# Differential attention: scores of two units in a row, packed into three PSUM banks per unit

## The chip, the cores and the metric

The program runs on one core of one Trainium2 chip. The metric is the device time of one execution in microseconds (us), the median of several. The core has five engines that this text speaks of by the profile's names: PE (TensorE; its weight loads are listed apart as PEld), DVE (VectorE), ACT (ScalarE), POOL (GpSimd) and SP (which issues DMAs). Each works through its own instructions in order, and they are tied to one another by semaphores.

## The reference, cut to what matters

The program computes two whole networks, one after the other: two layers of a first block (retention, sparse attention, gating, feed-forward), and then two layers of a second (gated delta rule, feed-forward, differential attention, feed-forward). The change lies in differential attention alone. There, each of 8 heads has two score maps with 64 numbers per key; the second map's softmax is subtracted from the first's with a learned factor, and the difference weighs the values.

```python
DA_HEADS = 8; DA_DIM = 64; DA_QBLOCK = 128        # 512 queries, 512 + 256 keys
k_all = jnp.concatenate([kl, kc], axis=3)
v_all = jnp.concatenate([vl, vc], axis=2)

def attend(q, k, v):
    s = jnp.einsum('cbhqd,cbhkd->cbhqk', q, k).astype(f32)   # c: the two maps
    p = jax.nn.softmax(s, axis=-1)
    a = p[0] - lam_val * p[1]
    return jnp.einsum('bhqk,bhkv->bhqv', a, v.astype(f32))
```

All of it is float32, and what comes out is 512 x 1024 numbers.

## The kernel before, in words

The program is a row of stages. Each stage has one function per engine (`da_pe`, `da_act`, `da_dve`, `da_pool` for the stage of this text), written out by hand in the order in which that engine shall work; a stage ends with a barrier (`stage_end`) at which the stage's semaphores are cleared. No planner decides anything. Queries, keys and values lie in SBUF when the stage begins, and the stage issues no DMA.

The stage has 32 units (`AUNITS`, L3596): 8 heads times 4 blocks of 128 queries. For each unit u the steps are these.

- **Scores** (`scores`, L3607 to 3619, PE): four matmuls, two maps times the keys in pieces of 512 and 256. A map has 64 rows to contract, so map 0 uses the upper 64 rows of the array and map 1 the lower 64. Each float32 matmul appears in the trace as two passes. A map of a unit has a buffer of two PSUM banks, and there are three such buffers (`da_scores`, L3655): one and a half units.
- **Lowest** (`lowest`, L3696, DVE): the queries were scaled by a negative number, so the smallest of 768 scores is wanted, for each map.
- **Exp** (L3680, ACT): the exponential of a map, with its sum over the keys read out behind it. The sum signals `p_ready`, which frees the score buffer. The results lie in SBUF, in one of three buffers (`k.ap`).
- **Factor and combination**: DVE forms the reciprocals of the two sums (L3716) and the factor of the second map (L3717). Then DVE adds factor times map 1 to map 0 for keys 0 to 383 (L3724), and POOL does so for keys 384 to 767 in two instructions (L3738 a product, L3739 a sum).
- **Turn** (`turn`, L3629, PE): the combination is transposed in two halves of three 128 x 128 blocks. Both halves go into the same PSUM bank, bank 6, so each turn waits until ACT has copied the one before it out (`turned_half`, L3670, signalling `pt_ready`).
- **Weigh** (`weigh`, L3638, PE): six matmuls with the values, into bank 7. DVE scales the result (L3703) and sums its squares (L3710).

PE's order in one round u is scores(u), first turn of u-2, weigh(u-3), second turn of u-2. ACT's order is copy of the first turn of u-2, exp of map 0 of u, exp of map 1 of u, copy of the second turn of u-2. DVE's order is the scaling of u-4, lowest of map 0, squares of u-4, reciprocals and factor of u-1, lowest of map 1, combination of u-1.

Of the kernel before, what the change touches and what calls it, by code (L numbers as in the profile page):

```python
# [25 lines left out]
P = 128  # L26
# [114 lines left out]
class Semaphores:  # L141


    def __init__(self, nc):
        sem = nc.alloc_semaphore
# [22 lines left out]
        self.o_taken = sem("o_taken")  # L168
        self.vsq_ready = sem("vsq_ready")
        self.p_ready = sem("p_ready")  # L170
        self.factor_ready = sem("factor_ready")
        self.s_ps = sem("s_ps")
        self.ov_taken = sem("ov_taken")
# [378 lines left out]
def spin_pe(k, pe, moving, bank, n):  # L552

    for _ in range(n):
        signal_later(k, pe.matmul(k.ps[:, bank, :], k.ident, moving, start=True, stop=True))
# [1559 lines left out]
SEGS = ((0, 512, 0), (512, 256, 516))  # L2115
# [1481 lines left out]
KEYS = NT2 * P  # L3597
# [5 lines left out]
def da_pe(k, e, slot, _):  # L3603
    pe, S = e.eng, k.S
    n = len(AUNITS)

    def scores(u):  # L3607
        h, i = AUNITS[u]
        if u >= 2:
            pe.wait_ge(S.p_ready, 2 * u - 1)  # L3610
        elif u == 1:
            pe.wait_ge(S.p_ready, 1)
        for at, m, _ in SEGS:
            for c in range(2):
                rows = slice(64 * c, 64 * c + 64)
                last = pe.matmul(da_scores(k, u, c)[:, at:at + m], k.aq[rows, h, i * P:(i + 1) * P],  # L3616
                                 k.ak[rows, h, at:at + m], start=True, stop=True)
                if at:
                    last.then_inc(S.s_ps, 1)

    def turn(v, part):
        if part == 0:
            pe.wait_ge(S.combined, v + 1)
            pe.wait_ge(S.combined_pool, v + 1)
        if v or part:
            pe.wait_ge(S.pt_ready, 2 * v + part)
        for j in range(3):
            at = HALF_KEYS * part + j * P
            last = pe.transpose(k.ps[:, 6, j * P:(j + 1) * P], k.ap[v % 3][:, 0, at:at + P], k.ident)  # L3629
        last.then_inc(S.pt_ps, 1)  # L3630

    def weigh(v):
        h, i = AUNITS[v]
        pe.wait_ge(S.pt_ready, 2 * v + 2)
        if v:
            pe.wait_ge(S.ov_taken, v)
        for j in range(NT2):
            last = pe.matmul(k.ps[:, 7, 0:P], k.apt[v % 2][:, j * P:(j + 1) * P], k.av[:, j, h * P:(h + 1) * P],  # L3638
                             start=j == 0, stop=j == NT2 - 1)
        last.then_inc(S.ov_ps, 1)  # L3640

    spin_pe(k, pe, k.c2[:, 0:512], 7, 1)
    for u in range(n + 3):
        if u < n:
            scores(u)
        if 2 <= u < n + 2:
            turn(u - 2, 0)
        if u >= 3:
            weigh(u - 3)
        if 2 <= u < n + 2:  # L3650
            turn(u - 2, 1)
    spin_pe(k, pe, k.c2[:, 0:512], 0, 3)


def da_scores(k, u, c):  # L3655

    b = 2 * ((2 * u + c) % 3)
    return k.ps[:, b:b + 2, :].rearrange("p a b -> p (a b)")[:, 0:KEYS]


def da_act(k, e, _):
    act, S = e.eng, k.S
    n = len(AUNITS)

    def turned_half(v, part):
        act.wait_ge(S.pt_ps, 2 * v + part + 1)
        if v >= 2 and part == 0:
            act.wait_ge(S.ov_ps, v - 1)
        at = HALF_KEYS * part
        act.activation(k.apt[v % 2][:, at:at + HALF_KEYS], k.ps[:, 6, 0:HALF_KEYS], ACT.Copy).then_inc(S.pt_ready, 1)  # L3670

    for u in range(n + 2):
        for c in range(2):
            if u >= 2 and c == 0:
                turned_half(u - 2, 0)
            if u < n:
                act.wait_ge(S.o_ps, 2 * u + c + 1)
                if u >= 3 and c == 0:
                    act.wait_ge(S.pt_ps, 2 * (u - 2))
                act.activation(k.ap[u % 3][:, c, :], da_scores(k, u, c), ACT.Exp, bias=k.amin[:, 2 * u + c:2 * u + c + 1],  # L3680
                               scale=-1.0, accum_out=k.asum[:, 2 * u + c:2 * u + c + 1]).then_inc(S.p_ready, 1)
            if u >= 2 and c == 1:
                turned_half(u - 2, 1)
    act.activation(k.small[:, 254:255], k.eps, ACT.Sqrt)
    act.wait_ge(S.head_ms_ready, 1)
    act.activation(k.small[:, 64:64 + 8 * NT1], k.small[:, 64:64 + 8 * NT1], ACT.Sqrt).then_inc(S.head_std_ready, 1)


def da_dve(k, e, _):
    dve, S = e.eng, k.S  # L3690
    n = len(AUNITS)

    def lowest(u, c):
        at = 2 * u + c
        dve.wait_ge(S.s_ps, at + 1)
        dve.tensor_reduce(k.amin[:, at:at + 1], da_scores(k, u, c), AX.X, ALU.min).then_inc(S.o_ps, 1)  # L3696

    for u in range(n + 4):
        if u >= 4:
            v = u - 4  # L3700
            h, i = AUNITS[v]
            dve.wait_ge(S.ov_ps, v + 1)
            dve.tensor_scalar(k.amix[:, i, h * P:(h + 1) * P], k.ps[:, 7, 0:P], k.arec[:, 2 * v:2 * v + 1],  # L3703
                              None, ALU.mult).then_inc(S.ov_taken, 1)
        if u < n:
            lowest(u, 0)
        if u >= 4:
            unit = k.amix[:, i, h * P:(h + 1) * P]
            dve.wait_ge(S.ov_taken, v + 1)
            dve.tensor_tensor_reduce(out=k.asq, in0=unit, in1=unit, scale=1.0, scalar=0.0, op0=ALU.mult, op1=ALU.add,  # L3710
                                     accum_out=k.small[:, 8 * i + h:8 * i + h + 1]).then_inc(S.head_sq_summed, 1)
        if 1 <= u <= n:
            v = u - 1
            rec, fac = k.arec[:, 2 * v:2 * v + 2], k.afac[:, v:v + 1]
            dve.wait_ge(S.p_ready, 2 * v + 2)
            e.link(dve.reciprocal(rec, k.asum[:, 2 * v:2 * v + 2]))  # L3716
            dve.scalar_tensor_tensor(fac, rec[:, 1:2], k.asum[:, 2 * v:2 * v + 1], k.lamt[:, 133:134],  # L3717
                                     ALU.mult, ALU.mult).then_inc(S.factor_ready, 1)
        if u < n:
            lowest(u, 1)  # L3720
        if 1 <= u <= n:
            p = k.ap[v % 3][:, :, 0:HALF_KEYS]
            dve.wait_ge(S.factor_ready, v + 1)
            dve.scalar_tensor_tensor(p[:, 0, :], p[:, 1, :], fac, p[:, 0, :], ALU.mult, ALU.add).then_inc(S.combined, 1)  # L3724
    part = 1.0 - LAMBDA_INIT
    dve.wait_ge(S.head_sq_summed, n)
    dve.tensor_scalar(k.small[:, 64:64 + 8 * NT1], k.small[:, 0:8 * NT1], 1.0 / (P * part ** 2), EPS / part ** 2, ALU.mult,
                      ALU.add).then_inc(S.head_ms_ready, 1)
    dve.wait_ge(S.head_std_ready, 1)
    dve.reciprocal(k.small[:, 0:8 * NT1], k.small[:, 64:64 + 8 * NT1])  # L3730
# [280 lines left out]
```

## Time and profile before

| what | value |
|---|---|
| median of 3 runs | 3542.41 us (3542.16 to 3545.89) |
| the profiled execution | 3539.66 us |
| its span in the trace | 3537.9 us |
| the stage of the change, from its first scores to the barrier's end | 2961.3 to 3094.0, 132.7 us |
| busy in that stretch: PE, DVE, ACT, POOL | 120.5, 102.1, 91.5, 66.9 us |
| granted TensorE clock in that stretch, share of full speed | 1.00 |

The profile is of one execution. Its own time stands beside its span because 1.8 us of it lie before the first and behind the last instruction that the trace has. Times within the trace count from the span's start. PE's busy time includes the drain of each matmul, which lies beside the next matmul; so how long PE needs for a step is read from the start of one group of matmuls to the start of the next.

### The profile page before, as it was taken

To read this page: it belongs to the slowest core of one execution; us is meant where nothing else is said; L and a number is where in the kernel's file an instruction comes from. 1 tells how busy PE (TensorE), PEld (TensorE's weight loads), DVE (VectorE), ACT (ScalarE), POOL (GpSimd) and SP (SyncE) were. 2 spreads that over 40 slices of the span, in tenths; PEclk is the share of its full clock that TensorE was granted. 3 is DMA by queue.
4 is the path that set the end of the run, shared out by engine and by line. 5 is a ranking of instruction groups with operands and counts; after the bars stand their busy time and mean duration, and the time that the engine had idled before them with its cause. 6 is when DMAs were issued, how large, how long until landed. Compare 5 with 4: busy or idle time off the path is not lost.

```text
span 3537.9 us, 57598 instructions
## 1 busy us (share of the span) xinstructions
PE 3409.8 (96%) x24652; PEld 2813.1 (80%) x24652; DVE 2083.2 (59%) x2894; ACT 823.1 (23%) x1551; POOL 341.6 (10%) x311
## 2 busy tenths in 40 slices
PE   8999999999999999999998999999999999999998
PEld 6777888877778888878888977888888686678886
DVE  4665777746657776756665666422245754764347
ACT  1243001222530012542252221000021204610021
POOL 0000000000100000025205500300000002502000
PEclk9999999999999999999999999999999999999999
DMA  4311544423025443210010041111111331022222
GB/s 177 109 37 50 206 186 165 147 95 108 25 77 196 185 160 124 105 38 3 32 60 3 4 161 60 60 60 61 71 60 72 112 111 36 1 84 95 97 100 90
DMA packets 51454, 320.48 MB, mean 91 GB/s; under 512 B 7132, under 2 KB 7644, under 8 KB 16648
## 3 DMA queue, kind: packets, MB, share of 16 engines
q1 hardware_dynamic: 30492, 220.50, 17.0%
q10 hardware_dynamic: 20716, 96.36, 7.6%
q8 instruction: 195, 3.19, 0.4%
q14 instruction: 51, 0.42, 0.0%
HBM read 299.94 MB, written 9.56 MB: 87 GB/s over the span
## 4 chain that ended last, share of the span: by engine, by line
PE 79%; DVE 7%; PEld 6%; DMA 3%; issue 2%; ACT 2%; PEldq 1%; POOL 0%; POOLq 0%; ACTq 0%; another core or an unknown queue 0%; DVEq 0%; SPq 0%
PE psum L561 20%; PE psum L562 20%; PE psum L563 20%; PE psum L2633 4%; PE psum L2640 3%; DMA pieces_in<-pieces 2%; PEld psum L561 2%; PEld psum L563 2%; PEld psum L562 2%; PE psum L1404 1%; PE psum L1388 1%; PE psum L758 1%; PE psum L1377 1%; PE psum L3616 1%; DVE xt_values L3696 1%
## 5 line engine op out<-in xcount | busy, mean ns | idle before, releaser
L561 PE MATMUL psum<-xt_operands,pieces_hi 128*128 128x512 f32 (+1 forms) x2544 | 938.6, 369 | 19.4 <-DVE xt_operands L818 8.4
L562 PE MATMUL psum<-xt_operands,pieces_hi 128*128 128x512 f32 (+1 forms) x2544 | 927.9, 365 | 0.0
L563 PE MATMUL psum<-xt_operands,pieces_lo 128*128 128x512 f32 (+1 forms) x2544 | 927.1, 364 | 0.0
L561 PEld LDWEIGHTS psum<-xt_operands,pieces_hi 128*128 128x128 f32 x2544 | 480.9, 189 | 106.7 <-issue 15.2
L561 PE MATMUL psum<-pieces_hi,xt_operands 128*128 128x512 f32 x1338 | 532.2, 398 | 15.5 <-DVE pieces_lo L608 10.6
L563 PEld LDWEIGHTS psum<-xt_operands,pieces_lo 128*128 128x128 f32 x2544 | 480.8, 189 | 77.2
L562 PEld LDWEIGHTS psum<-xt_operands,pieces_hi 128*128 128x128 f32 x2544 | 481.3, 189 | 73.4
L562 PE MATMUL psum<-pieces_lo,xt_operands 128*128 128x512 f32 x1338 | 524.5, 392 | 0.0
L563 PE MATMUL psum<-pieces_hi,xt_operands 128*128 128x512 f32 x1338 | 524.2, 392 | 0.0
L618 DVE TENSOR_TENSOR pieces_lo<-pieces_in,pieces_hi 128x2048 fp32r<-128x2048 f32 x190 | 443.5, 2334 | 5.3
L575 DVE CAST pieces_hi<-pieces_in 128x2048 fp32r<-128x2048 f32 x190 | 237.5, 1250 | 301.6 <-PE psum L561 154.6
L561 PEld LDWEIGHTS psum<-pieces_hi,xt_operands 128*128 128x128 f32 x1338 | 253.4, 189 | 74.7 <-DVE pieces_lo L608 12.6
L562 PEld LDWEIGHTS psum<-pieces_lo,xt_operands 128*128 128x128 f32 x1338 | 253.6, 190 | 54.3 <-issue 2.4
L563 PEld LDWEIGHTS psum<-pieces_hi,xt_operands 128*128 128x128 f32 x1338 | 253.5, 189 | 53.6
L1667 ACT ACTIVATE arena<-psum 128x512 f32<-128x512 f32 x66 | 39.5, 598 | 673.8 <-PE psum L563 673.8
L1703 DVE TENSOR_TENSOR arena<-psum,arena 128x512 f32<-128x512 f32 x66 | 45.6, 691 | 247.1 <-ACT arena L1667 247.1
L3460 DVE TENSOR_TENSOR arena<-psum,arena 128x768 f32<-128x768 f32 x22 | 21.1, 957 | 256.1 <-ACT arena L3427 256.1
L2442 DVE SCALAR_TENSOR_TENSOR x_mem<-x_mem,arena 128x772 f32<-128x772 f32 x96 | 98.2, 1023 | 66.8 <-ACT x_mem L2341 64.2
L2633 PE MATMUL psum<-arena 128*128 128x128 f32 x976 | 129.2, 284 | 0.0
L2633 PEld LDWEIGHTS psum<-arena 128*128 128x128 f32 x976 | 115.7, 193 | 6.1 <-DVE x_mem L2910 3.1
L1770 DVE SCALAR_TENSOR_TENSOR arena<-x_mem,xt_values,arena 128x2048 f32<-128x2048 f32 x44 | 101.9, 2345 | 3.3 <-DMA x_mem<-ada 3.3
L1684 ACT ACTIVATE xt_operands<-arena 128x512 fp32r<-128x512 f32 x102 | 59.8, 625 | 184.4 <-PE psum L561 145.0
(391 smaller groups left out, 4048.0 us busy)
## 6 DMA issues: line engine op xcount, KB each, us to landing
pieces_in<-pieces SPq DMA_DIRECT2D x210, 1024.0 KB, 4.8
x_mem<-ada ACTq DMA_DIRECT2D x28, 1024.0 KB, 4.9
arena<-ada ACTq DMA_DIRECT2D x20, 1024.0 KB, 4.8
arena<-mods ACTq DMA_DIRECT2D x8, 512.0 KB, 15.7
arena<-arena ACTq DMA_DIRECT2D x32, 128.0 KB, 4.9
xt_values<-arena ACTq DMA_DIRECT2D x8, 384.0 KB, 9.1
x_park<-x_mem ACTq DMA_DIRECT2D x1, 3072.0 KB, 14.4
o_park<-arena ACTq DMA_DIRECT2D x2, 1536.0 KB, 5.1
```

What stands on the lines that cost most here:

```text
L561: signal_later(k, pe.matmul(out, sh, mh, start=start, stop=False))
L562: signal_later(k, pe.matmul(out, sh, ml, start=False, stop=False))
L563: return pe.matmul(out, sl, mh, start=False, stop=stop)
L575: e.link(dve.tensor_copy(k.hi[n % 2], k.ring[i]))
L618: e.eng.tensor_tensor(k.ring_lo[i], k.ring[i], k.hi[n % 2].bitcast(F32), ALU.subtract).then_inc(k.S.lo_ready, 1)
L1667: act.activation(silu[:, f % 2, 0:nt * P], k.ps[:, 2 * (f % 2), 0:nt * P], ACT.Silu).then_inc(S.silu_ready, 1)
L1684: act.activation(hs[j % len(hs)][0], hid[:, j % FT, :], ACT.Copy).then_inc(S.hs_hi_ready, 1)
L1703: dve.tensor_tensor(hid[:, f, 0:nt * P], k.ps[:, 2 * (f % 2) + 1, 0:nt * P], silu[:, f % 2, 0:nt * P], ALU.mult).then_inc(S.hid_taken, 1)
L1770: eng.scalar_tensor_tensor(total, weights, c, total, ALU.mult, ALU.add).then_inc(added, 1)
L2442: ins = dve.scalar_tensor_tensor(conv, raw[:, j:j + 772], taps[:, n, j:j + 1], conv, ALU.mult, ALU.add)
L2633: last = pe.matmul(out, lhs(s, d, h), rhs(s, d, h), start=True, stop=True)
L2640: last = pe.matmul(out[r, h, :], lhs(h, r), rhs(h, r), start=True, stop=True)
```

## The change

Three things are altered, all in this stage.

The score buffers: a unit now has three PSUM banks, banks 0 to 2 or 3 to 5, in turn. The 768 scores of map 0 are followed at once by the 768 of map 1, so the middle bank is shared: its first half belongs to map 0, its second to map 1. Two units fit, and both maps of a unit are handed on together: the first lowest and the first exp of a unit wait for both maps (`s_ps` and `o_ps` at 2u+2), and the scores of u wait for both exps of u-2.

The order of a unit's matmuls: map 0's 512 keys, map 1's 256 (which fall into the middle bank), map 1's 512, map 0's 256 (also the middle bank). Before the last, PE waits on a new semaphore until map 1's 256 have been written.

The order of the steps: PE does the scores of units p and p+1, and then first turn, weigh, second turn of p-2 and of p-1. DVE does both lowest of a unit next to each other, ahead of the squares. ACT's order is as it was.

```diff
     def scores(u):
+
         h, i = AUNITS[u]
         if u >= 2:
-            pe.wait_ge(S.p_ready, 2 * u - 1)
-        elif u == 1:
-            pe.wait_ge(S.p_ready, 1)
-        for at, m, _ in SEGS:
-            for c in range(2):
-                rows = slice(64 * c, 64 * c + 64)
-                last = pe.matmul(da_scores(k, u, c)[:, at:at + m], k.aq[rows, h, i * P:(i + 1) * P],
-                                 k.ak[rows, h, at:at + m], start=True, stop=True)
-                if at:
-                    last.then_inc(S.s_ps, 1)
+            pe.wait_ge(S.p_ready, 2 * u - 2)
+        for c, at, m in ((0, 0, 512), (1, 0, 256), (1, 256, 512), (0, 512, 256)):
+            rows = slice(64 * c, 64 * c + 64)
+            if (c, at) == (0, 512):
+                pe.wait_ge(S.middle_bank_written, u + 1)
+            last = pe.matmul(da_scores(k, u, c)[:, at:at + m], k.aq[rows, h, i * P:(i + 1) * P],
+                             k.ak[rows, h, at:at + m], start=True, stop=True)
+            if at:
+                last.then_inc(S.s_ps, 1)
+            elif c == 1:
+                last.then_inc(S.middle_bank_written, 1)
...
-    for u in range(n + 3):
-        if u < n:
-            scores(u)
-        if 2 <= u < n + 2:
-            turn(u - 2, 0)
-        if u >= 3:
-            weigh(u - 3)
-        if 2 <= u < n + 2:
-            turn(u - 2, 1)
+    for pair in range(0, n + 2, 2):
+        if pair < n:
+            scores(pair)
+            scores(pair + 1)
+        for v in (pair - 2, pair - 1):
+            if v >= 0:
+                turn(v, 0)
+                if v >= 1:
+                    weigh(v - 1)
+                turn(v, 1)
+    weigh(n - 1)
...
-    b = 2 * ((2 * u + c) % 3)
-    return k.ps[:, b:b + 2, :].rearrange("p a b -> p (a b)")[:, 0:KEYS]
+    b = 3 * (u % 2)
+    return k.ps[:, b:b + 3, :].rearrange("p a b -> p (a b)")[:, KEYS * c:KEYS * c + KEYS]
...
-                act.wait_ge(S.o_ps, 2 * u + c + 1)
+                act.wait_ge(S.o_ps, 2 * u + 2)
...
-        dve.wait_ge(S.s_ps, at + 1)
+        dve.wait_ge(S.s_ps, 2 * u + 2)
...
         if u < n:
             lowest(u, 0)
+            lowest(u, 1)
...
-        if u < n:
-            lowest(u, 1)
```

On PE, one round in the middle of the stage stood in this order before (L3616 scores, L3629 a turn, L3638 a weigh; every wait is in brackets, a row with x2 or x5 holds the rest of its group):

```order
L3616 MATMUL psum<-arena 128x512 [waits p_ready]
L3616 MATMUL psum<-arena 128x512
L3616 MATMUL psum<-arena 128x256 x2
L3629 MATMUL psum<-arena,xt_values 128x128 [waits pt_ready,combined_pool,combined]
L3629 MATMUL psum<-arena,xt_values 128x128 x2
L3638 MATMUL psum<-arena,xt_values 128x128 [waits ov_taken,pt_ready]
L3638 MATMUL psum<-arena,xt_values 128x128 x5
L3629 MATMUL psum<-arena,xt_values 128x128 [waits pt_ready]
L3629 MATMUL psum<-arena,xt_values 128x128 x2
```

Now the same place reads as follows, from the second unit's scores of a pair on (L3617 scores, L3632 a turn, L3641 a weigh):

```order
L3617 MATMUL psum<-arena 128x512 [waits p_ready]
L3617 MATMUL psum<-arena 128x256
L3617 MATMUL psum<-arena 128x512
L3617 MATMUL psum<-arena 128x256 [waits middle_bank_written]
L3632 MATMUL psum<-arena,xt_values 128x128 [waits pt_ready,combined_pool,combined]
L3632 MATMUL psum<-arena,xt_values 128x128 x2
L3641 MATMUL psum<-arena,xt_values 128x128 [waits ov_taken,pt_ready]
L3641 MATMUL psum<-arena,xt_values 128x128 x5
L3632 MATMUL psum<-arena,xt_values 128x128 [waits pt_ready]
L3632 MATMUL psum<-arena,xt_values 128x128 x2
L3632 MATMUL psum<-arena,xt_values 128x128 [waits pt_ready,combined_pool,combined]
L3632 MATMUL psum<-arena,xt_values 128x128 x2
```

The second turn of one unit is now followed at once by the first turn of the next, with no scores between them, and the wait for `pt_ready` of that first turn is for ACT's copy of the turn just ahead of it.

On DVE, one round stood in this order before (L3703 scaling, L3696 lowest, L3710 squares, L3716 and L3717 reciprocals and factor, L3724 combination):

```order
L3703 TENSOR_SCALAR xt_values<-psum,xt_values 128x128 [waits ov_ps]
L3696 TENSOR_REDUCE xt_values<-psum 128x1 [waits s_ps]
L3710 ISA xt_values,arena<-xt_values 128x128 [waits ov_taken]
L3710 ISA arena 128x1
L3716 RECIPROCAL xt_values<-xt_values 128x2 [waits p_ready]
L3717 SCALAR_TENSOR_TENSOR xt_values<-xt_values,arena 128x1 [waits dve_chain]
L3696 TENSOR_REDUCE xt_values<-psum 128x1 [waits s_ps]
L3724 SCALAR_TENSOR_TENSOR xt_values<-xt_values 128x384 [waits factor_ready]
```

Now it reads (L3708 scaling, L3701 lowest, L3716 squares, L3722 and L3723 reciprocals and factor, L3728 combination):

```order
L3708 TENSOR_SCALAR xt_values<-psum,xt_values 128x128 [waits ov_ps]
L3701 TENSOR_REDUCE xt_values<-psum 128x1 [waits s_ps] x2
L3716 ISA xt_values,arena<-xt_values 128x128 [waits ov_taken]
L3716 ISA arena 128x1
L3722 RECIPROCAL xt_values<-xt_values 128x2 [waits p_ready]
L3723 SCALAR_TENSOR_TENSOR xt_values<-xt_values,arena 128x1 [waits dve_chain]
L3728 SCALAR_TENSOR_TENSOR xt_values<-xt_values 128x384 [waits factor_ready]
```

The factor of the unit before, for which POOL waits, now stands behind both lowest of the new unit, and the combination stands right behind the factor.

## Rows read from the trace of the kernel before

**Rows 1.** The profile's page, its first line.

```profile
span 3537.9 us, 57598 instructions
```

**Rows 2.** Windows: stretch, length, busy per engine, granted clock, DMA share, GB/s.

```profile
2961.30:3094.00 132.70, 120.50 (x839) 86.33 (x838) 102.08 (x258) 91.49 (x195) 66.86 (x64) 1.00 0.01 5
2962.00:2970.00 8.00, 3.86 (x24) 1.67 (x20) 4.46 (x7) 3.86 (x8) 1.97 (x2) 1.00 0.05 22
```

**Rows 3.** Timeline about a round without a gap: start, duration, engine, line, what.

```profile
3014.14 1.56 PE L3616 MATMUL psum<-arena 64*128 64x512 f32 x8
...
3014.68 0.19 PEld L3616 LDWEIGHTS psum<-arena 64*128 64x128 f32 x2 [0.24 <-issue]
...
3015.11 0.19 PEld L3616 LDWEIGHTS psum<-arena 64*128 64x128 f32 x2 [0.23 <-issue]
...
3015.67 0.52 PE L3629 MATMUL psum<-arena,xt_values 128*128 128x128 f32 x3
3015.74 0.96 DVE L3696 TENSOR_REDUCE xt_values<-psum 128x1 f32<-128x768 f32 x1 [0.83 <-PE psum L3616]
...
3016.03 1.50 PE L3638 MATMUL psum<-arena,xt_values 128*128 128x128 f32 x12
3016.23 0.49 ACT L3670 ACTIVATE xt_values<-psum 128x384 f32<-128x384 f32 x1 [0.70 <-PE psum L3629]
3016.61 0.28 DVE L3710 CUSTOM_DVE_ANT_0 xt_values<-xt_values 128x128 f32<-128x128 f32 x1
...
3016.82 0.16 DVE L3716 RECIPROCAL xt_values<-xt_values 128x2 f32<-128x2 f32 x1
3017.01 0.22 DVE L3717 SCALAR_TENSOR_TENSOR xt_values<-xt_values,arena 128x1 f32<-128x1 f32 x1
...
3017.37 0.49 PE L3629 MATMUL psum<-arena,xt_values 128*128 128x128 f32 x3
...
3017.79 0.70 PE L3616 MATMUL psum<-arena 64*128 64x512 f32 x2
```

**Rows 4.** Timeline about the round ahead of it, which has a gap on PE.

```profile
3010.16 1.56 PE L3616 MATMUL psum<-arena 64*128 64x512 f32 x8
...
3010.51 0.90 ACT L3680 ACTIVATE xt_values<-psum,xt_values 128x768 f32<-128x768 f32 x1 [0.41 <-DVE xt_values L3696]
3010.59 1.26 POOL L3739 TENSOR_TENSOR xt_values<-xt_values 128x384 f32<-128x384 f32 x1
...
3011.40 0.48 ACT L3670 ACTIVATE xt_values<-psum 128x384 f32<-128x384 f32 x1
...
3012.03 0.52 PE L3629 MATMUL psum<-arena,xt_values 128*128 128x128 f32 x3 [0.30 <-ACT xt_values L3670]
...
3012.58 0.49 ACT L3670 ACTIVATE xt_values<-psum 128x384 f32<-128x384 f32 x1 [0.70 <-PE psum L3629]
...
3012.97 0.90 ACT L3680 ACTIVATE xt_values<-psum,xt_values 128x768 f32<-128x768 f32 x1
```

**Rows 5.** Timeline at the stage's start: the first scores, the first two lowest.

```profile
2961.37 1.56 PE L3616 MATMUL psum<-arena 64*128 64x512 f32 x8
...
2962.96 1.82 DVE L3696 TENSOR_REDUCE xt_values<-psum 128x1 f32<-128x768 f32 x2 [3.20 <-PE psum L3616]
```

**Rows 6.** Groups of instructions by line within the stage: busy us, mean ns.

```profile
L3724 DVE SCALAR_TENSOR_TENSOR xt_values<-xt_values 128x384 f32<-128x384 f32 x32 | 20.1, 629 | 0.0
```

**Rows 7.** Timeline at the stage's end: the last unit, and the last weigh.

```profile
3084.37 0.22 DVE L3717 SCALAR_TENSOR_TENSOR xt_values<-xt_values,arena 128x1 f32<-128x1 f32 x1
...
3084.63 1.28 DVE L3724 SCALAR_TENSOR_TENSOR xt_values<-xt_values 128x384 f32<-128x384 f32 x1
...
3084.67 0.83 POOL L3738 TENSOR_TENSOR xt_values<-xt_values 128x384 f32<-128x384 f32 x1 [0.57 <-DVE xt_values L3717]
...
3085.57 1.19 POOL L3739 TENSOR_TENSOR xt_values<-xt_values 128x384 f32<-128x384 f32 x1
...
3089.90 1.27 PE L3638 MATMUL psum<-arena,xt_values 128*128 128x128 f32 x9 [0.58 <-ACT xt_values L3670]
```

More of the change, by code:

```diff
@@ L170, in __init__ @@
         self.p_ready = sem("p_ready")
+        self.middle_bank_written = sem("middle_bank_written")
         self.factor_ready = sem("factor_ready")
```

## The prediction

> **What bounds the kernel now.** I read the page first: one execution spans 3537.9 us [rows 1]. The change touches one stage, so I cut it out with the view of windows: 132.7 us, in which PE is busy 120.5, DVE 102.1, ACT 91.5 and POOL 66.9 us [rows 2]. The reader is to see that PE is close to full there, but that no engine is far behind, so that the order of the steps can decide. The chain of waits was next: in this stretch it goes round through PE's scores, DVE's lowest, ACT's exp and copy, and PE's turn, weigh, turn, once in two rounds. The timeline then gives the steps. I count PE by the starts of its groups. In one round scores to turn takes 1.53 us (3014.14 to 3015.67), turn to weigh 0.36, weigh to turn 1.34, turn to the next scores 0.42: 3.65 us without a gap [rows 3]. The round ahead of it takes 3.98 us (3010.16 to 3014.14), since its first turn comes 0.30 us late, behind ACT's copy [rows 4]. Two rounds are 7.63 us. So before, PE does 7.30 us of work in 7.63, and what there is to win is that 0.33 and whatever the regrouping saves on PE.
>
> **What it removes.** The wait of scores for an exp of the unit just before goes, since two whole units now have buffers; in the middle of the stage it cost nothing that the rows show. Scores that follow scores lose the cost of going from whole-array work to half-array work and back. The passes of one piece of 512 keys start 0.43 us apart (3014.68 to 3015.11) [rows 3], a piece of 256 should take 0.21, and two passes of each make 1.28 us for a unit, the two maps side by side. So the first scores of a pair should take 1.28 instead of 1.53, and one turn-to-scores step of 0.42 becomes a turn-to-turn step of about 0.36. Gain per pair: 0.25 + 0.06 = 0.31 us.
>
> **The new matmul order inside a unit.** Each map still has 768 keys in two passes, so 1.28 us if both halves of the array stay busy. Map 0's last 256 keys wait for the semaphore of map 1's first 256, which should have been streamed after 0.43 us, while map 0's first 512 need 0.85. This wait is covered by about 0.4 us. The trace shows no wait of PE on its own matmul here, so bounds: below, 1.28 us, because the columns are the same; above, no overlap of the halves at all, 2.56 us. I take 1.28, nearest to the row in which eight passes fit into 1.56 us [rows 3].
>
> **What it adds.** In a pair, the second turn of unit p-2 is followed at once by the first turn of p-1, which uses the same bank 6. It cannot start until ACT has copied the second turn out, and scores no longer lie between. ACT's order is unchanged, and this is what makes the wait long: the copy of the second turn stands behind both exps of unit p, these stand behind the copy of the first turn of p-2, and that turn now stands behind the scores of two units. Counted from the start of the pair's first scores:
>
> - ACT's path: scores 1.28 + 1.53 = 2.81 to the first turn; turn to copy 0.56 (3015.67 to 3016.23) [rows 3]; copy to exp 0.39 (3012.58 to 3012.97), exp to the copy behind it 0.89 (3010.51 to 3011.40), which I also take for exp to exp, and copy to turn 0.63 (3011.40 to 3012.03) [rows 4]. Sum: 2.81 + 0.56 + 0.39 + 0.89 + 0.89 + 0.63 = 6.17 us.
> - DVE's and POOL's path. The same turn also waits until POOL has combined unit p-1. POOL waits for the factor, and DVE now makes that behind both lowest of unit p. Scores to lowest 1.60 (3014.14 to 3015.74) [rows 3]; two lowest take 1.82 with 0.95 for the last, so each holds DVE 0.87 [rows 5], together 1.74; squares to reciprocals 0.21, reciprocals to factor 0.19 [rows 3]; factor to POOL's product 0.30, product to sum 0.90 [rows 7]; the sum 1.26, and from its end to the turn at most 0.18 (3011.85 to 3012.03) [rows 4]. There ACT's copy ended 0.03 us later than POOL, so I take 0.15. Sum: 1.60 + 1.74 + 0.21 + 0.19 + 0.30 + 0.90 + 1.26 + 0.15 = 6.35 us.
>
> The later one decides: the second unit's first turn at 6.35 us. PE would be ready for it at 2.81 + 0.36 + 1.34 + 0.36 = 4.87, so it stands idle for 1.48 us. Behind it 0.36 + 1.34 + 0.42 = 2.12, and the next pair begins at 8.47 us. Against 7.63 that is 0.84 us more for each pair. Queued on PE behind that waiting turn are a weigh, a turn and the next pair's scores, and for these wait DVE's next lowest, and so everything.
>
> **Side costs.** DVE's combination now starts right behind the factor, beside POOL's product. At the stage's end, where the order happens to be that, it took 1.28 us (3084.63); the mean of all 32 is 629 ns, so the other 31 took (32 x 0.629 - 1.28) / 31 = 0.61 us [rows 6, 7]. I expect about 1.28 us for all 32. It costs nothing by itself: the combination is not on POOL's path, and it is followed by the next unit's lowest, whose exps ACT reaches only at about 7.3 us. DVE then has per pair four lowest of 0.87 and twice about 2.3 us of the rest, some 8.1 of 8.47, so it is nearly full; if it grew by 0.4 us it would be the bound. PE's clock: in the stage's first 8 us, with PE busy for 3.86 of them, the granted clock stayed at 1.00, the level of 2.4 GHz [rows 2]; an idle 1.48 us in 8.47 should leave it there.
>
> **The sum.** Fill, from the same steps: exps of unit 0 at 3.5 and 4.3, scores 2 at 5.4 (an exp of 0.90 and a hand-over of 0.14), exps of unit 1 at 5.2 and 6.1, scores 3 at 7.1, first turn 8.7, copy 9.2, exps of unit 2 at 9.6 and 10.5, copy 11.4, turn of unit 1 at 12.0, scores 4 at 14.2 us. Then 13 pairs to scores 30: 13 x 8.47 = 110.1. Then the end, counted from scores 30: factor of unit 30 at 7.8 (behind a combination of 1.28 from 4.0 on, a scaling and two lowest), POOL's sum done at 10.3, its turns at 10.4 and 12.1, copy and turn of unit 31 at 12.7 and 13.3, its second turn 15.0, copy 15.6, last weigh 16.2. Together 14.2 + 110.1 + 16.2 = 140.5 us from first scores to last weigh. Before it is 3089.90 - 2961.37 = 128.5 us [rows 5, 7]. So +12.0 us. The profiled execution took 3539.66 us and should become 3551.7; it lies 2.8 us under the median of the runs shown, 3542.41, against which I forecast 3554.4 us.
>
> **Rivals.**
>
> *The scores lose their side-by-side.* For it: in-order issue, and a wait in the middle of the unit that was not there. Against it: the cover of 0.4 us. If map 0's last 256 keys came wholly by themselves, 0.43 us for each scores, ACT's path would be 6.17 + 0.86 = 7.03 and the pair 9.15: 13 x 1.52 + 3 = 23 us, 3565 us. With no overlap at all: 6.17 + 2.56 = 8.73, the pair 10.85, about +49 us, 3591 us. Chance 12%.
>
> *DVE and POOL hold each other longer than the combination shows.* If the squares too were held by the 0.67 us that the combination loses (1.28 against 0.61), POOL's path would be 7.02 and the pair 9.14: 13 x 0.67 = 8.7 more, 3563 us. Against it: the squares stand where POOL should be idle. Chance 8%.
>
> *Only bank 6 counts.* If the copy of the second turn found ACT free, the second unit's turn would come at 2.81 + 0.36 + 1.34 + 0.56 + 0.63 = 5.70, the pair at 7.82: 13 x 0.19 and about 1 us for fill and end, +3.5 us, 3546 us. It needs both paths 0.5 to 0.7 us shorter than their rows. Chance 7%.
>
> *Faster: PE was the bound, and the regrouping pays.* If the second unit's turn did not wait at all, a pair would be 4.87 + 2.12 = 6.99 us, 0.64 less than now: 16 x 0.64 = 10 us, 3532 us. It decides as soon as the idle time ahead of that turn is under 0.64 us instead of 1.48. For it: PE is the fullest engine, and half of the changes between half-array and whole-array work go. Against it: even a free ACT leaves 5.70 - 4.87 = 0.83 us of idle time, for the bank alone. Chance 4%. The Trainium skill (TensorEngine Tiling (Array Packing), Key Properties) says that a change of tiling mode drains TensorE. By that rule alone the change must win, since it halves the changes of mode. The rows agree on a cost, but a small one: scores to turn is 1.53 where the passes make 1.28, of which some is the first weight load [rows 3].
>
> **How the numbers follow.** The forecast has 69%. Its own range: the pair between 8.29 (ACT's path alone) and 8.65 (scores of 1.40), thus +9.5 to +14.5 us, and with 2 us for the scatter of the runs 3550 to 3559. The range for 8 in 10 goes up to the first of the rivals and down a little, 3548 to 3565 us. About 0.2% (7 us) is what a measurement of this kernel can tell from no change. Slower by more than that: forecast less a small part, and the first two rivals, 88%. Within it: the third rival and a little, 8%. Faster: 4%.
>
> **What would show it.** Right, step by step: in the middle of the stage scores to scores 1.28 us inside a pair and a pair of 8.47; the second unit's first turn idle for about 1.5 us, released by ACT's copy or POOL; the copy of second turns directly behind the second exp of an even unit; combinations of about 1.28 us; the granted clock at 1.00. The stage's first scores to last weigh should be 140.5 us and every other stage as before. Wrong: a pair under 7.9 us, or idle time ahead of the second unit's turn of less than 0.8 us; scores to scores over 1.6 us would point to the first rival.

## The result, and the profile after

The changed kernel takes 3565.57 us (median of 5 runs, 3561.94 to 3573.47), the kernel before 3545.89 us beside it (5 runs, 3542.16 to 3552.71). The ratio is 1.0057, with a 95% interval of 1.0038 to 1.0076: slower, by about 20 us. The forecast was 3554.4 us with a range up to 3565; counted as a rise it was 12.0 us, and 19.7 were measured.

The profiled execution took 3565.57 us, 25.9 more than that of before. Two stretches hold the difference. In the changed stage, first scores to last weigh is 3115.63 - 2967.24 = 148.4 us where before had 128.5, so +19.9. Another 6.2 us lie in an early stage that the change does not touch (all the rest together is 0.2 us shorter). The view of windows shows that stage, before first and then after (columns as in [rows 2]):

```profile
878.50:984.60 106.10, 100.37 (x962) 78.88 (x962) 66.98 (x264) 51.40 (x126) 12.35 (x28) 1.00 0.09 31
```

```profile
878.30:990.60 112.30, 106.62 (x962) 84.40 (x962) 67.04 (x264) 51.39 (x126) 12.40 (x28) 0.94 0.08 29
```

The same 962 matmuls and the same work on DVE, ACT and POOL, but a granted clock of 0.94 instead of 1.00. That is scatter of one execution: three of the changed kernels below (wait kept with its own bank, old order, spin matmuls) had 1.00 in this stage. And the ratio of the medians, worth 20 us, agrees with the changed stage alone. So all that follows is read inside the stage.

The timeline of the changed kernel shows a pair of units in the middle of the stage, the answer to [rows 3, 4] (start, duration, engine, line, what, and in brackets the idle time before and what ended it; L3617 scores, L3632 a turn, L3675 its copy, L3685 exp, L3743 POOL's sum):

```profile
3019.19 0.73 PEld L3617 LDWEIGHTS psum<-arena 64*128 64x128 f32 x6 [0.17 <-ACT xt_values L3685]
3019.19 3.52 PE L3617 MATMUL psum<-arena 64*128 64x512 f32 x16
...
3020.39 0.83 PEld L3617 LDWEIGHTS psum<-arena 64*128 64x128 f32 x8 [0.46 <-PE psum L3617]
...
3022.02 0.29 PEld L3617 LDWEIGHTS psum<-arena 64*128 64x128 f32 x2 [0.80 <-PE psum L3617]
...
3022.64 0.55 PE L3632 MATMUL psum<-arena,xt_values 128*128 128x128 f32 x3
...
3023.23 0.49 ACT L3675 ACTIVATE xt_values<-psum 128x384 f32<-128x384 f32 x1 [2.96 <-PE psum L3632]
...
3023.61 0.90 ACT L3685 ACTIVATE xt_values<-psum,xt_values 128x768 f32<-128x768 f32 x1
...
3024.47 1.19 POOL L3743 TENSOR_TENSOR xt_values<-xt_values 128x384 f32<-128x384 f32 x1
...
3025.37 0.50 ACT L3675 ACTIVATE xt_values<-psum 128x384 f32<-128x384 f32 x1
...
3026.01 0.52 PE L3632 MATMUL psum<-arena,xt_values 128*128 128x128 f32 x3 [1.15 <-ACT xt_values L3675]
...
3028.12 3.52 PE L3617 MATMUL psum<-arena 64*128 64x512 f32 x16
```

The pair is 3028.12 - 3019.19 = 8.93 us; two rounds of before took 7.63. ACT stands idle for 2.96 us until the first turn comes; then copy, exp, exp (the second, at 3024.49, not shown) and copy follow without a wait, and the second unit's first turn waits for the last of them, 6.82 us after the pair's first scores. That is the chain the prediction drew, but the first turn, which starts it, comes 3.45 us after the start of the scores and not 2.81.

Where the 0.64 us are is seen on the weight loads. The view of waits over the stage sums them (engine and line, what it waited for, us in total, times, longest):

```profile
PEld psum L3617 <- PE psum L3617: 20.5, 32, 0.8
```

Once in each of the 32 scores the weight loads stand still until a matmul of the same scores is done, 0.64 us on average (in the pair above 0.46 and 0.80). (That this is also the 0.64 us that a pair lost is chance; what one wait costs is worked out below.) Before, the loads of the scores waited only 0.23 us at a time for their issue, and stood at the start of each pass [rows 3]. The load that stands still is the one for map 0's last 256 keys, so the wait is the new one, for the middle bank.

Three more groups answer to rows of before. The combination, by line within the stage [rows 6, 7]:

```profile
L3728 DVE SCALAR_TENSOR_TENSOR xt_values<-xt_values 128x384 f32<-128x384 f32 x32 | 41.1, 1284 | 1.1
```

All 32 take 1.28 us, where before one did. The fill, in PE's timeline and in the windows:

```profile
2967.24 3.52 PE L3617 MATMUL psum<-arena 64*128 64x512 f32 x16
2972.96 5.10 PE L3617 MATMUL psum<-arena 64*128 64x512 f32 x16 [2.19 <-ACT xt_values L3685]
2977.98 0.55 PE L3632 MATMUL psum<-arena,xt_values 128*128 128x128 f32 x3
```

```profile
2967.20:2973.00 5.80, 3.61 (x19) 1.84 (x18) 3.61 (x5) 1.97 (x5) 0.00 (x0) 1.00 0.20 86
2973.00:2976.40 3.40, 3.40 (x11) 2.25 (x13) 1.68 (x4) 1.67 (x4) 2.02 (x2) 0.50 0.00 0
2990.00:3100.00 110.00, 95.91 (x645) 71.35 (x647) 94.57 (x199) 65.42 (x149) 49.45 (x50) 1.00 0.01 1
```

After two units' scores and 2.19 us of idle time, the granted clock falls to 0.50, the level of 1.2 GHz, for the stretch from 2973.0 to 2976.4, and the second pair's scores take 5.02 us to the turn (2972.96 to 2977.98) instead of 3.45. In the middle of the stage the clock is 1.00. And the stage's end:

```profile
3115.63 1.60 PE L3641 MATMUL psum<-arena,xt_values 128*128 128x128 f32 x12 [0.58 <-ACT xt_values L3675]
```

From scores 30 at 3099.59 that is 16.04 us.

### The profile page after: what moved, and what is told of

Its sections match the earlier page's. It is cut to its first block, busy times and chain, and to the rows that moved or that the text cites. A ratio compares the mean times of both kernels' runs of the same rounds, so it can differ in the third digit from the quotient of the medians.

```text
span 3563.8 us, 57598 instructions
## 1 busy us (share of the span) xinstructions
PE 3423.2 (96%) x24652; PEld 2825.4 (79%) x24652; DVE 2105.9 (59%) x2894; ACT 818.0 (23%) x1551; POOL 339.5 (10%) x311
## 4 chain that ended last, share of the span: by engine, by line
PE 79%; DVE 6%; PEld 6%; DMA 3%; issue 2%; ACT 2%; PEldq 1%; POOL 0%; POOLq 0%; ACTq 0%; another core or an unknown queue 0%; DVEq 0%; SPq 0%
PE psum L562 20%; PE psum L564 20%; PE psum L563 20%; PE psum L2634 4%; PE psum L2641 3%; DMA pieces_in<-pieces 2%; PEld psum L562 2%; PEld psum L564 2%; PEld psum L563 2%; PE psum L3617 2%; PE psum L1405 1%; PE psum L1389 1%; PE psum L759 1%; PE psum L1378 1%; PEldq L503 1%
## 5 line engine op out<-in xcount | busy, mean ns | idle before, releaser
L562 PEld LDWEIGHTS psum<-xt_operands,pieces_hi 128*128 128x128 f32 x2544 | 480.9, 189 | 106.4 <-issue 15.2
```

What stands on the lines that cost most here:

```text
L562: signal_later(k, pe.matmul(out, sh, mh, start=start, stop=False))
```

## The experiments

The first four ask what makes the scores longer, and what a pair costs without each suspect. "The pair" is read in the middle of each stage, from one pair's first scores to the next's.

**The wait taken away.** Map 0's last 256 keys are written over the first bank, which map 0 owns anyway, so no wait is needed:

```diff
-            if (c, at) == (0, 512):
-                pe.wait_ge(S.middle_bank_written, u + 1)
+            to = 0 if (c, at) == (0, 512) else at
-            last = pe.matmul(da_scores(k, u, c)[:, at:at + m], ...
+            last = pe.matmul(da_scores(k, u, c)[:, to:to + m], ...
```

> The changed kernel, but map 0's last 256 keys are written over the first 256 columns of map 0's own bank instead of into the middle bank, and the wait on the middle bank's semaphore is gone, since no bank is shared any more. (256 scores of map 0 are so not computed into their place.) Theory A, the wait on PE's own matmul costs about 0.34 us in each scores: scores to scores in a pair goes from 1.73 back to 1.28 us, the pair from 8.93 to about 8.45, first scores to last weigh from 148.4 to about 139.5 us, which is what was forecast. Theory B, the order of the pieces (512, 256, 512, 256 instead of like beside like) keeps the two halves of the array from working side by side: scores to scores stays at 1.7 and the stage at 148 us.

PE's timeline of this kernel (L3616 scores, L3631 a turn, L3742 POOL's sum):

```profile
3033.60 2.85 PE L3616 MATMUL psum<-arena 64*128 64x512 f32 x16
3036.38 0.55 PE L3631 MATMUL psum<-arena,xt_values 128*128 128x128 f32 x3
...
3039.87 0.52 PE L3631 MATMUL psum<-arena,xt_values 128*128 128x128 f32 x3 [1.28 <-POOL xt_values L3742]
...
3041.99 0.69 PE L3616 MATMUL psum<-arena 64*128 64x512 f32 x2
```

Two scores to the turn take 2.78 us (forecast 2.81), the second unit's first turn comes at 6.27 and is now released by POOL (forecast 6.35, by POOL), and the pair is 8.39 (forecast 8.47). First scores to last weigh is 140.0 us, where the prediction had 140.5. So with this one wait gone the middle of the stage is close to the forecast, and the miss there sits in the wait. That the whole stage agrees to 0.5 us is in part luck: 13 pairs that are each 0.08 shorter make up for a fill that is 1.0 longer.

**The wait kept, the shared bank not used.** As above, but the two removed lines stay.

> As the first run of this call, no bank shared, but the wait for the semaphore of map 1's first 256 keys is kept ahead of map 0's last 256. (256 scores of map 0 are so not computed into their place.) Theory A, it is the wait itself: all as in the changed kernel, scores to scores 1.73, pair 8.93, stage 148.4 us. Theory C, two halves of the array that write into one bank hold each other: without the shared bank scores to scores 1.3 and the stage about 139.5 us, although the wait is there.

```profile
3033.14 3.52 PE L3618 MATMUL psum<-arena 64*128 64x512 f32 x16
3036.59 0.55 PE L3633 MATMUL psum<-arena,xt_values 128*128 128x128 f32 x3
...
3042.07 2.42 PE L3618 MATMUL psum<-arena 64*128 64x512 f32 x12
```

3.45 us to the turn and a pair of 8.93, as in the complete change, with no bank shared by the two maps. It is the wait that costs, not the bank. (First scores to last weigh is 151.2 us, 2.9 more than after; the excess lies in the fill and the pair behind it, while the clock fell twice; from scores 6 on the pairs are 8.93 again.)

**The wait kept, but for something long done.** The same again, with a wait for the middle bank of the unit before:

```diff
-                pe.wait_ge(S.middle_bank_written, u + 1)
+                pe.wait_ge(S.middle_bank_written, max(u, 1))
```

> As the run with its own bank and the wait kept, but the wait is for the unit before (count u instead of u+1, for the first unit 1), so that it is long satisfied when PE comes to it. (256 scores of map 0 are not computed into their place.) Theory A1, what costs 0.34 us is a wait that is still open when PE comes to the load: now the pair is about 8.4 us and first scores to last weigh about 140 us, as with no wait. Theory A2, any wait on a semaphore between matmuls of the two halves keeps the load from being made ahead: the pair stays at 8.93 and the stage at 148 us.

```profile
3035.11 2.85 PE L3618 MATMUL psum<-arena 64*128 64x512 f32 x16
3037.89 0.55 PE L3633 MATMUL psum<-arena,xt_values 128*128 128x128 f32 x3
...
3043.50 1.98 PE L3618 MATMUL psum<-arena 64*128 64x512 f32 x10
```

2.78 us and a pair of 8.39: a wait that is already met costs nothing. Only one that is open when PE comes to it does.

In the changed kernel the second pass of map 0's 512 keys starts at 3019.73, where the timeline of PE alone, asked for from 3019.9 on, begins:

```profile
3019.73 2.99 PE L3617 MATMUL psum<-arena 64*128 64x512 f32 x13
```

The wait for the load of the next weights ends at 3020.39, 0.66 us later, where in [rows 3] the load stands at the pass's start (3014.68). The pass should last 0.43 (spacing of the passes, [rows 3]), so 0.23 us of idle time and some 0.1 us of a load that nothing covers are left: by this estimate about 0.34 for each scores, half of 3.45 - 2.78.

Why the wait is open at all can be read from the times at which semaphores are set, which the trace keeps too. The semaphore of map 1's first 256 keys is set at 3020.35, 1.15 us after the start of the scores, and at 1.15 us also in the two kernels that do not wait for it there (3034.75 - 3033.60 without a wait, 3036.27 - 3035.11 with the old one). The second pass of these 256 keys starts at 3019.52 and its record ends at 3019.90. What ends just ahead of 3020.35 is the second pass of map 0's 512 keys (3019.73 + 0.59 = 3020.32), and these keys stand ahead of map 1's 256 in PE's order. In each of the 32 units of all nine packed kernels of this text the semaphore is set 0.01 to 0.03 us after the record of a pass of 512 keys ends, and 0.45 us or more after that of its own pass ends. (The ends of matmuls are modelled in the profile.) So PE signals as if in its order: this wait is in effect one for map 0's own 512 keys, the piece that was to cover it. In the kernel with the old wait the load for map 0's last 256 keys stands 0.54 us into the scores and their first pass 0.96 us, both ahead of 1.15.

The Trainium skill (TensorE: Matmul & The Clock Gate, "Step-by-step: what each phase is for") says that TensorE pulls a weight load ahead of matmuls still running when the row groups do not conflict or the load goes to the background weight buffer. The rows of before agree (the load at 3014.68 stands beside passes that have only begun); what the three kernels add is that this stops at a load whose wait is open.

**The packing in the old order.** PE goes back to one unit per round; the three banks and the new wait stay:

```diff
-    for pair in range(0, n + 2, 2):
...
+    for u in range(n + 3):
+        if u < n:
+            scores(u)
+        if 2 <= u < n + 2:
+            turn(u - 2, 0)
+        if u >= 3:
+            weigh(u - 3)
+        if 2 <= u < n + 2:
+            turn(u - 2, 1)
```

> The changed kernel with PE's order of before: scores of u, first turn of u-2, weigh of u-3, second turn of u-2; packing, piece order, waits and DVE's order stay changed. Theory A, the packing by itself costs most of it (both lowest ahead of the factor, exps only after both maps, and the wait in each scores), and the pairing adds little: two units about 8.76 us and first scores to last weigh about 145 us. Theory D, the loss is the pairing, that is the second turn and the next first turn side by side without scores between them: two units 7.63 plus twice 0.34, about 8.3 us at most, first scores to last weigh under 139 us.

```profile
3033.12 1.89 PE L3617 MATMUL psum<-arena 64*128 64x512 f32 x8
3035.69 0.52 PE L3632 MATMUL psum<-arena,xt_values 128*128 128x128 f32 x3 [0.68 <-POOL xt_values L3741]
...
3037.81 1.89 PE L3617 MATMUL psum<-arena 64*128 64x512 f32 x8
3039.68 0.52 PE L3632 MATMUL psum<-arena,xt_values 128*128 128x128 f32 x3
...
3041.80 0.69 PE L3617 MATMUL psum<-arena 64*128 64x512 f32 x2
```

Two units take 8.68 us, 1.05 more than before, and first scores to last weigh 144.2. Scores to turn, without waiting, is 1.87 (3037.81 to 3039.68) instead of 1.53: the 0.34 again, in both rounds. The rest is a turn in every other round that POOL releases 0.68 us late, where before one came 0.30 late; a likely reason, not tested by itself here, is that DVE now makes the factor behind both lowest. The packing alone costs most of the change; doing two units in a row adds 0.25 us a pair.

**ACT's order.** For even units the second turn's copy goes between the two exps, so that the second unit's first turn need not wait for the second exp:

```diff
+            if u >= 2 and c == 1 and u % 2 == 0:
+                turned_half(u - 2, 1)
...
-            if u >= 2 and c == 1:
+            if u >= 2 and c == 1 and u % 2 == 1:
```

> The changed kernel, but for even units ACT copies the second turn between the two exps instead of behind both. ACT's path to the second unit's first turn is so 0.89 us shorter. Theory A, POOL's path stands right behind it (6.62 against 6.82 us from the pair's start): the turn is then released by POOL, the pair is about 8.75 us and first scores to last weigh about 144 us. Theory E, ACT's order is the only thing that holds the turn: the pair is about 8.05 us and the stage about 135 us.

```profile
3032.84 3.52 PE L3617 MATMUL psum<-arena 64*128 64x512 f32 x16
...
3039.40 0.52 PE L3632 MATMUL psum<-arena,xt_values 128*128 128x128 f32 x3 [0.90 <-POOL xt_values L3745]
...
3041.52 0.70 PE L3617 MATMUL psum<-arena 64*128 64x512 f32 x3
```

The pair is 8.68 and POOL now ends the wait, at 6.56 us. So POOL's path stands 0.25 us behind ACT's in the changed kernel, and mending ACT's order alone is worth no more than that.

**All three taken out.** The first edit (map 0's last 256 in its own bank, no wait), ACT's order as just shown, and on DVE, in even rounds, the factor ahead of everything (the steps became functions, which are left out here; odd rounds keep the changed kernel's order):

```diff
+        steps = "factor scale low0 low1 squares combine" if u % 2 == 0 else "scale low0 low1 squares factor combine"
```

> The changed kernel with three things taken away at once: map 0's last 256 keys go over its own bank (no bank shared, no wait; these 256 scores are not computed into their place); ACT copies the second turn of an even unit between the two exps; and in even rounds DVE makes the factor before the two lowest instead of behind them, with the combination behind the squares. Theory A (two paths, ACT's and POOL's, each held the second unit's first turn): both are now about 0.9 to 1.7 us shorter, and only bank 6's own round trip and ACT are left: a pair of 7.75 to 8.0 us, first scores to last weigh 129 to 132 us, near the kernel before. Theory F, pairing needs more than the paths that were named: the pair stays over 8.3 us and the stage over 138 us.

```profile
3019.63 2.85 PE L3616 MATMUL psum<-arena 64*128 64x512 f32 x16
...
3024.14 0.49 PE L3631 MATMUL psum<-arena,xt_values 128*128 128x128 f32 x3
3025.30 0.52 PE L3631 MATMUL psum<-arena,xt_values 128*128 128x128 f32 x3 [0.67 <-ACT xt_values L3674]
...
3027.42 1.98 PE L3616 MATMUL psum<-arena 64*128 64x512 f32 x10
```

The pair is 7.79 us, first scores to last weigh 131.0. What is left is bank 6: from the second turn to the next unit's first it takes 1.16 us, and PE is idle for 0.67 of them, until the copy is done. That is the rival that only the bank counts (7.82), and it is still above the 7.63 of before. So in this order of steps, with both turns in one bank, two units in a row did not win even without the three waits; another order of the turns was not tried.

**The clock in the fill.** Spin matmuls in the first idle gap, to keep PE busy there:

```diff
             scores(pair + 1)
+            if pair == 0:
+                spin_pe(k, pe, k.c2[:, 0:512], 7, 2)
```

> The changed kernel with two matmuls of 512 columns, whose result nobody reads, behind the scores of the first pair, where PE otherwise idles for 2.2 us. Theory G, the idle time is why the granted clock fell to 1.2 GHz for 3.4 us there and the second pair's scores took 5.02 instead of 3.45 us: the clock stays at 1.00 in the fill, and first scores to last weigh is about 1.6 us shorter, 146.8 us. Theory H, the clock's fall has nothing to do with that idle time: it falls all the same and the stage stays at about 148.4 us.

```profile
2975.48 0.52 PE L3632 MATMUL psum<-arena,xt_values 128*128 128x128 f32 x3 [1.69 <-ACT xt_values L3677]
2975.84 2.72 PE L3641 MATMUL psum<-arena,xt_values 128*128 128x128 f32 x12
```

```profile
2975.00:2980.00 5.00, 4.52 (x23) 4.09 (x24) 2.59 (x5) 3.08 (x7) 2.02 (x2) 0.66 0.00 0
```

The first two rows are PE's timeline, the third a window about them. The second pair's scores now took 3.59 us to the turn, and the clock fell after them: to a mean of 0.66 over these 5 us, and the first weigh took 2.72 us instead of 1.50. First scores to last weigh is 148.5 us, nothing won. That the first idle gap makes it fall is therefore not shown. Idle time is not ruled out either, since PE had stood idle for 1.69 us just ahead of this fall. It fell in the fill of every packed kernel here, and in neither that of before nor that of the kernel that follows; what decides it stays open.

**The other way round: the kernel before, with DVE's order alone changed.** Since POOL waits for DVE's factor in all of these kernels, the factor goes ahead of both lowest in every round of the kernel before, and the squares go to the end. PE, ACT and POOL keep their order:

```diff
+        steps = "scale factor low0 low1 combine squares"
```

> The kernel before with one change, DVE's order in a round: scaling, reciprocals and factor, lowest of map 0, lowest of map 1, combination, squares. It takes up what the chain of before and these runs point to: the factor, for which POOL waits, and the second lowest, for which ACT's exp and copy wait, both come earlier. Theory A: PE's gap of 0.30 us in every second round goes, two rounds take 7.30 instead of 7.62 us, and first scores to last weigh about 123.5 instead of 128.5 us; the whole about 5 us faster. Rival: the squares, which now stand beside POOL's sum, are held by it (0.7 instead of 0.28 us) and push DVE's next round back: 128 us or more, no gain.

> The kernel before with DVE's order scaling, reciprocals and factor, lowest of map 0, lowest of map 1, combination, squares, now timed in rounds against the kernel before. In one look its stage went from 128.5 to 123.3 us, while stages that are the same in both took longer in that execution. Theory A: the other stages scatter from run to run, and the rounds show the 5.2 us, a ratio of about 0.9985 with an interval that may still reach 1. Rival: the new order costs time elsewhere, and the ratio is 1 or above.

A single run took 3548.39 us, with two units at 7.27 and first scores to last weigh at 123.3 us instead of 128.5. The stages ahead of this one took 13 us longer in that execution than in the profiled one of before, so its total says nothing. Timed, the kernel takes 3537.91 us (median of 11 runs) against 3544.36 (15 runs) of the kernel before, a ratio of 0.9984, interval 0.9975 to 0.9993: faster by about 6 us, where the stage shows 5.2 (123.3 again). Its timeline (L3616 scores, L3696 lowest, L3629 a turn, L3715 factor, L3721 combination, L3751 and L3752 POOL's product and sum):

```profile
3012.43 0.22 DVE L3715 SCALAR_TENSOR_TENSOR xt_values<-xt_values,arena 128x1 f32<-128x1 f32 x1
3012.73 0.83 POOL L3751 TENSOR_TENSOR xt_values<-xt_values 128x384 f32<-128x384 f32 x1 [1.73 <-DVE xt_values L3715]
...
3012.97 1.82 DVE L3696 TENSOR_REDUCE xt_values<-psum 128x1 f32<-128x768 f32 x2 [0.31 <-PE psum L3616]
...
3013.64 1.00 POOL L3752 TENSOR_TENSOR xt_values<-xt_values 128x384 f32<-128x384 f32 x1
...
3014.71 0.61 DVE L3721 SCALAR_TENSOR_TENSOR xt_values<-xt_values 128x384 f32<-128x384 f32 x1
...
3015.01 1.56 PE L3616 MATMUL psum<-arena 64*128 64x512 f32 x8
...
3016.51 0.55 PE L3629 MATMUL psum<-arena,xt_values 128*128 128x128 f32 x3
...
3018.65 1.56 PE L3616 MATMUL psum<-arena 64*128 64x512 f32 x8
```

The factor is done before the lowest begin, POOL starts 0.3 us behind it, and in the middle of the stage no turn waits any more: scores to turn is 1.50, a round 3.64, and the gap of [rows 4] is gone. Whether it is the factor or the second lowest, which also comes earlier, was not taken apart.

**The complete change with both orders mended.** The changed kernel, with ACT's and DVE's edits from above:

> The changed kernel, complete, with its middle bank and wait as they are, but with ACT's copy of an even unit's second turn between the two exps and, in even rounds, DVE's factor ahead of the two lowest and the combination behind the squares. It tells how much of the loss the two orders give back without touching the packing. Theory A: ACT's path is the longer again, 3.45 to the first turn, then 0.56 + 0.39 + 0.89 of ACT to the copy and 0.63 to the turn: 5.92, at 2.12 for the rest a pair of 8.0 to 8.4 us, first scores to last weigh 135 to 140 us, ratio to before 1.002 to 1.0035. Rival, the wait in each scores is by itself what keeps it slow: the pair stays at 8.7 us or more and the stage at 144 us.

```profile
3032.23 3.52 PE L3617 MATMUL psum<-arena 64*128 64x512 f32 x16
...
3037.41 0.49 PE L3632 MATMUL psum<-arena,xt_values 128*128 128x128 f32 x3
3038.57 0.52 PE L3632 MATMUL psum<-arena,xt_values 128*128 128x128 f32 x3 [0.67 <-ACT xt_values L3675]
...
3040.68 1.68 PE L3617 MATMUL psum<-arena 64*128 64x512 f32 x7
```

3557.75 us (5 runs), a ratio of 1.0039, interval 1.0024 to 1.0054; the pair is 8.45 and first scores to last weigh 141.2 us, each a little over what was expected. The turn waits for bank 6 alone, at 6.34: second turn at 5.18, copied and turned 1.16 later. The scores' 0.67 and the bank's 0.67 remain, and the kernel stays slower than before.

## Why the prediction was right in kind and too small

Direction and place came out, and so did the larger part of the mechanism: slower, in this stage, through the second unit's first turn, which waits behind ACT's order with POOL's path close to it. That the regrouping is the cause came out in part only: with PE in its old order the packed kernel already lost 15.7 of the 19.9 us (144.2 against 128.5). By the prediction's own steps:

| step | forecast | measured after | without the wait |
|---|---|---|---|
| two scores to first turn | 2.81 | 3.45 | 2.78 |
| ACT's path to the second unit's turn | 6.17 | 6.82 | |
| POOL's path to the same turn | 6.35 | 6.57 | 6.27 |
| idle time of PE ahead of it | 1.48 | 1.15 | 1.28 |
| from that turn to the next pair | 2.12 | 2.11 | 2.12 |
| the pair | 8.47 | 8.93 | 8.39 |
| fill | 14.2 | 16.2 | 15.2 |
| end | 16.2 | 16.0 | 15.8 |
| first scores to last weigh | 140.5 | 148.4 | 140.0 |

(POOL's path after is its sum's start, 5.28, and the 1.29 from sum to turn of the kernel without the wait.)

- **The step that failed** is the price of the new matmul order inside a unit. The prediction put the wait of map 0's last 256 keys at nothing: map 1's 256 "should have been streamed after 0.43 us", map 0's 512 keys need 0.85, so the wait was "covered by about 0.4 us". The semaphore is set at 1.15 us, when map 0's 512 keys are done, and not at 0.43; without an open wait the keys that stand behind it start at 0.96 and their load at 0.54. So there was no cover, and the held load comes on top. Measured, this costs 0.34 us a scores. So ACT's path grew by 0.65 (6.82 against 6.17), passed POOL's, and the pair by 0.46: 13 x 0.46 = 6.0 us of the 7.9 that are missing.
- **The first rival had the cause** (the scores lose part of their side-by-side), with 0.43 us a scores where 0.34 was measured, and it was given 12%. Its sign, scores to scores over 1.6 us, came true with 1.73. That its 3565 us is so near to the 3565.57 measured is luck in part: it adds 23 us to 3542.41, and the rise was 19.7 over 3545.89. No row of before had a load that may not start until a matmul has ended, since in [rows 3] each pass has its load at its start; so the value at the cheap bound had less support than it was given.
- **The fill** was 2.0 us longer than forecast: 1.6 of it are the second pair's scores at half clock (5.02 against 3.45), and the other 0.4 was not taken apart. The prediction argued the clock from 3.86 of 8.00 us busy at 1.00 [rows 2], and for the middle of the stage that held; for the fill, which the sum takes at full clock, it did not.
- **A bound that does not come out of its working:** the pair of 8.65 with "scores of 1.40". Scores that are 0.12 longer make 8.53 by ACT's path and 8.59 by POOL's. It changes nothing, as 8.93 lies outside either.
- **Right as put:** the combination at 1.28 us for all 32, the 2.12 behind the turn, the end, the granted clock of 1.00 in the middle, and the gain of scores that follow scores, seen where the wait is gone: 2.78 for two (2.81 forecast), where twice 1.53 [rows 3] would be 3.06. The rival "only bank 6 counts" was priced right too (7.82 against 7.79 with the other waits taken out), and so was the refusal of a gain: even then a pair is longer than before.

## What to carry to other kernels

Price a new wait on an engine by when its semaphore is really set, and by what it holds up in the queue. Here the semaphore came when the piece ahead of it in PE's order was done, so that this piece could not cover the wait; and a wait that is open when a weight load reaches it also ends the load's head start. Put such a wait where it is long met, or give the operand its own place. When work is regrouped, follow the buffer that is still single (here one bank for every turn) and the order of the engines that were left alone. A reorder of DVE by itself, the factor ahead of two reductions and the squares last, made the kernel before faster, while the regrouping stayed slower even with its three waits taken out.

## What the runs showed of the hardware that was not expected

The semaphore of a matmul of 256 keys on one half of the array was set only when the 512 keys on the other half, ahead of it in PE's order, were done: 1.15 us into the scores, 0.45 us after its own record ended (3020.35 in the changed kernel).

An open wait ahead of a half-array matmul costs 0.34 us a scores; the same wait already met costs nothing (pairs of 8.93 and 8.39).

DVE's combination takes 0.61 us where nothing of POOL's runs beside it (3014.71 in the kernel with the factor first) and 1.28 us where POOL's product starts 0.04 us behind it and runs beside it. The Trainium skill (GPSIMD Engine Reference, "Specifications") says that GpSimd shares its SBUF interfaces with VectorE and that VectorE instructions with two SBUF inputs contend with it. The trace agrees: the combination has two such inputs. It also shows that either engine can pay. POOL's product keeps its 0.83 us beside the combination. POOL's sum does not: it took 1.00 us with no combination beside it (factor first), 1.19 with 0.33 us of it (after) and 1.26 with 0.41 us of it (before), where the combination still took 0.61. What decides which of the two is held was not tested.

The granted clock fell to 0.50 in the fill of each packed kernel, also where PE's first idle gap was filled.
